# Gate columns from a stream with stationary weights, and softmax rows scaled on GpSimd in the neighbourhood attention

## The chip, the cores and the metric

The kernel runs on one core of a Trainium2 chip. The metric is device time in microseconds (us), median of the runs: 3284.68 us before (3 runs, 3283.81 to 3284.96). One further execution was profiled; the trace is of that one.

## What is computed

Two blocks follow one another on 256 tokens of width 2048, all in float32. The first is a transformer block (SwiGLU, grouped and differential attention, SwiGLU). The second has two layers; the change is in these. Layer 0 works on 256 image tokens and 256 context tokens (four tiles of 128 tokens), layer 1 updates only the image tokens (two tiles). What matters of the reference:

```python
p = h @ w_in                       # h: normed tokens; p holds pool, q, k, v, gate b, conv, gate c
s_loc = einsum(q_r, k_win) + bias  # 8 x 16 window, 16 heads of 64
s_ctx = einsum(q_r, kc)            # 256 context keys
p_ = softmax(concatenate([s_loc, s_ctx]))
na = einsum(p_loc, v_win) + einsum(p_ctx, vc)
yb = na * silu(p[..., OFF_B_G:OFF_C_U])          # the gate of the attention, 1024 columns
yc = conformer_conv(p[..., OFF_C_U:OFF_C_G]) * silu(p[..., OFF_C_G:])
x_new = x + gate * (concatenate([ya, yb, yc]) @ w_out)
```

The context tokens of layer 0 attend to the 256 context keys alone (no window).

## The kernel before

Every large product is done in three matmuls of a split float32 (fp32r): high activations by high weights, low by high, high by low. A weight piece is 128 x 512. `hi_piece` on ScalarE rounds it, `lo_piece` on VectorE makes the remainder, TensorE uses both. The ring has four pieces, and ScalarE and VectorE run two pieces ahead (`LOOK`). In `chunk_pieces` the activations are the stationary operand (128 x 128, `hT`) and the weights move (512 columns, lines 456, 457 and 461). One chunk has 16 pieces and yields 512 output columns for `nt` token tiles in `nt` PSUM banks.

In each layer `ly` of the second block the streams of `SEGS` come in the order q, k, v, g, two chunks each. `take4` (line 1779) copies each finished bank to `qkvg` (token rows, columns free); `tap` adds one tap of the depthwise convolution (line 1774) on VectorE for each piece. The gate g is thus held by token rows in `qkvg[:, 3]`. After the streams ScalarE, in its program order, turns the convolution's result into columns (four copies, line 1065, after the last taps), applies Silu to the whole gate (line 1071) and takes a square root (line 1073). TensorE runs some filling matmuls on `ones` (`fill`, line 1984), waits for the four copies (`cv_turned`) and transposes the convolution's result (line 2406). From there the layer norm of the convolution (VectorE line 1785 and on), the pointwise product (line 2425) and the attention follow.

The attention goes over 8 pairs of heads. A group `g` has two units `u = 2g, 2g+1`, one per head, for one tile of queries; a pair has three groups in layer 0 (`G = 3`; the third, `t == 2`, holds both context tiles, 256 queries) and two in layer 1 (`G = 2`). All engines run a hand-written software pipeline, one `step(g)` for each group:

- TensorE: `staged` for the next pair at one step in `G` (line 2437), `na_scores(g + 1)` (lines 2450 to 2459), `na_turn(2g)` and `na_turn(2g + 1)` (line 2471: the exponentials are transposed), `na_gate(g - 1)` (line 2481: the gate, already divided by the softmax sum, is transposed), `na_values(g - 1)` (lines 2493 and 2500).
- VectorE: `na_gate(g - 1)` (reciprocal of the sums, line 1834; gate times reciprocal, line 1837), `take_q` at one step in `G` (line 1801), `na_max(2g + 2)` and `na_max(2g + 3)` (lines 1817 and 1823: scores plus bias, row maximum), `na_out(g - 1)` (line 1846: copy of the transposed gate, line 1849: product with the values' result).
- ScalarE: `take_k` (line 1088), `na_exp(2g + 2)` and `na_exp(2g + 3)` (lines 1094 and 1099), `na_pt(2g)` and `na_pt(2g + 1)` (line 1108: transposed exponentials to SBUF).
- GpSimd issues DMAs and clears a few tiles (line 2662 clears `nil`, 128 x 256, just ahead of each attention). It has no part in the steps.

Each engine executes its queue in order. `na_turn(u)` waits for `p_made`, the exponential of its unit, and nothing else but a free PSUM bank. After the last group `o_hi` and `o_low` split the gated result into `hT` for the output stream `o2`.

Of the kernel before, what the change touches and what calls it, by code (L numbers as in the profile page):

```python
# [17 lines left out]
F32 = mybir.dt.float32  # L18
# [97 lines left out]
def build(nc, a, out, xs_dram):  # L116
    ctx = ExitStack()
    with ctx:
# [4 lines left out]
            ca_const_in glu_made gates_made yt_done yt_taken pl_done pl_taken py_done py_taken pad_made  # L123
            conv_step cf_in cf_done z_made cz_done s_made pw_done yc_made na_in bias_in nil_made rot_made
            st_dve pt_done pt_taken gs_done gs_taken x4r_in fin_in y_out gate_diag rs_made cf_sd zt_done zt_taken w_made og_in s_diag sbc_done mods_made y1_made sig_made ag_made gc_made hq_made tq_done tq_taken
            vw_in cv_turned tmp_made y_made gr_made gt_done gt_taken""".split()
# [52 lines left out]
        qkvg = at("qkvg", Q, [P, 4, 4, 2 * CH])  # L179
        ca = at("ca", Q, [P, 5, 4, CH])  # L180
# [82 lines left out]
        def phase(name, pieces, taken, groups, fulls=0, turns=None):  # L263
            phases[name] = Phase(*total)
            for k, n in enumerate((pieces, taken, groups, fulls, groups if turns is None else turns)):
# [20 lines left out]
                [("q", 0, 2, 2), ("k", 2, 2, 4), ("v", 4, 2, 4), ("g", 6, 2, 2)]]  # L286
# [114 lines left out]
        def head_rows(nt, n):  # L401

            k = kt_of(n) - 4
            return qkvg[:, 3, 0:nt, k * P:(k + 1) * P]

        def tok_tiles(v):

            return v.rearrange("p (t n) -> p t n", n=P)
# [282 lines left out]
        def _(act):  # L691
# [330 lines left out]
            for ly in range(2):  # L1022
# [36 lines left out]
                for k, (nm_, _, n_, _) in enumerate(SEGS[ly]):  # L1059
                    stream(phases[f"s{ly}{nm_}"].pieces, n_, after=gate_c if k == 0 else None)  # L1060

# [8 lines left out]
                act.wait_ge(S["acc_taken"], phases[f"mx{ly}"].taken)  # L1070
                act.activation(qkvg[:, 3, 0:nt], qkvg[:, 3, 0:nt], ACT.Silu).then_inc(S["gates_made"], 1)
# [61 lines left out]
                def o_hi(n, ly=ly, nt=nt):  # L1133
# [5 lines left out]
                    else:  # L1139
                        act.wait_ge(S["o_taken"], o_total(ly + 1))  # L1140
                        act.activation(tok_tiles(dst), head_rows(nt, n), ACT.Copy).then_inc(S["tg_hi"], 1)
# [43 lines left out]
        def _(dve):  # L1185
# [524 lines left out]
            for ly in range(2):  # L1710
# [55 lines left out]
                for nm_, c0, n_, snt in SEGS[ly]:  # L1766
# [9 lines left out]

                    def take4(i, t, c0=c0, nm_=nm_, snt=snt):
                        bank = acc[first_bank(snt, i + (nm_ == "q")) + t]
                        dve.tensor_copy(qkvg[:, c0 // 2, t, bass.ds(i * CH, CH)], bank[:]).then_inc(S["acc_taken"], 1)
# [47 lines left out]
                def na_gate(g):  # L1827

                    s, t = 2 * g % 4, kinds[2 * g % U][1]
                    n = 2 if t == 2 else 1  # L1830
                    dve.wait_ge(S["p_made"], 16 + u0 + 2 * g + 2)

                    wait(dve, "gr_made", v0 + g - 1)
                    link(dve.reciprocal(rr4[:, s:s + 2, 0:n], sm4[:, s:s + 2, 0:n]))
                    for k in range(n):
# [863 lines left out]
```

## Time and profile before

| | |
|---|---|
| median of 3 runs | 3284.68 us |
| the profiled execution | 3289.47 us |
| its span (first to last instruction) | 3287.6 us |
| granted TensorE clock, mean | 0.996 |
| stream g, layer 0 / layer 1 | about 87 us / 43 us |
| attention, layer 0 / layer 1 | 87.9 us (2443.1 to 2531.0) / 55.6 us (3125.9 to 3181.5) |

The times stand in microseconds from the start of the span. The profile names engines as PE (TensorE matmuls), PEld (weight loads), DVE (VectorE), ACT (ScalarE), POOL (GpSimd) and SP. A row names the line of the kernel, the operation, what is written and read, and the shape as partitions x elements. A float32 matmul that is not split appears as two rows of MATMUL (xcount is doubled), a split (fp32r) one or a transpose as one. Busy times of TensorE overlap, since matmuls are pipelined; the spacing of their starts says what one costs.

### The profile page before, as it was taken

The numbers are of one execution on the slowest core, as the hardware profiler recorded it, in microseconds if no ns is written. First come the engines' busy times: TensorE is split into PE (matmuls) and PEld (weight loads), VectorE is DVE, ScalarE is ACT, GpSimd is POOL, SyncE is SP. The second block draws the span as 40 slices with busy tenths as digits, with TensorE's granted clock in tenths as the row PEclk, the third lists the DMA queues.
The fourth block names the chain that finished last, engine by engine and source line by source line (L and its number), as shares of the span: only waits on it lengthen the run. The fifth ranks groups of instructions, "written<-read, shape, count | busy, mean of one in ns | idle before, by whom it ended". The sixth has DMA issues, their size and how long they took to land.

```text
span 3287.6 us, 41059 instructions
## 1 busy us (share of the span) xinstructions
PE 3235.8 (98%) x15334; PEld 2647.4 (81%) x15334; DVE 2262.9 (69%) x4132; ACT 1544.2 (47%) x2880; POOL 97.2 (3%) x186
## 2 busy tenths in 40 slices
PE   9999999999999999999999999999999999999998
PEld 7888888888888788888888788888866778888766
DVE  6888888877766788888877633556656337756666
ACT  6544454445665554455555522222246336522464
POOL 0000000000000000000000000000000000000000
PEclk9999999999999999999999999999999999999999
DMA  8888877776555788887887432333321235543625
GB/s 278 267 263 258 259 259 255 264 256 194 154 153 173 250 268 259 260 259 257 266 268 257 143 109 90 99 97 97 109 93 72 89 100 183 180 123 99 190 78 172
DMA packets 286023, 616.35 MB, mean 187 GB/s; under 512 B 18880, under 2 KB 21504, under 8 KB 284160
## 3 DMA queue, kind: packets, MB, share of 16 engines
q1 hardware_dynamic: 261792, 527.50, 50.2%
q0 software_dynamic: 22656, 82.78, 7.9%
q10 hardware_dynamic: 1376, 3.44, 0.3%
q8 instruction: 122, 2.00, 0.3%
q14 instruction: 77, 0.63, 0.1%
HBM read 605.26 MB, written 6.29 MB: 186 GB/s over the span
## 4 chain that ended last, share of the span: by engine, by line
PE 94%; DVE 2%; ACT 2%; DMA 2%; issue 1%; SPq 0%; ACTq 0%; DVEq 0%
PE acc L456 29%; PE acc L461 29%; PE acc L457 29%; PE tp L2471 1%; PE acc L2493 1%; PE tp L2425 1%; DMA raw<-ffn_w_gu 1%; PE tp L2034 1%; PE acc L2456 0%; PE cgw L2437 0%; DVE lo L451 0%; PE cgw L2187 0%; PE tp L1996 0%; PE cgw L2374 0%; PE cgw L2565 0%
## 5 line engine op out<-in xcount | busy, mean ns | idle before, releaser
L447 ACT ACTIVATE hi<-raw 128x512 fp32r<-128x512 f32 x1808 | 1134.0, 632 | 1551.2 <-PE acc L461 1438.2
L451 DVE TENSOR_TENSOR lo<-raw,hi 128x512 fp32r<-128x512 f32 x1808 | 1208.7, 689 | 835.4 <-ACT hi L447 826.3
L456 PE MATMUL acc<-hi,hT_hi 128*128 128x512 f32 x1760 | 696.5, 396 | 9.4 <-DVE hT_lo L1259 4.9
L457 PE MATMUL acc<-hi,hT_lo 128*128 128x512 f32 x1760 | 685.8, 390 | 0.0
L456 PE MATMUL acc<-hi,h_hi 128*128 128x512 f32 x1696 | 671.5, 396 | 7.9 <-ACT hi L447 4.5
L457 PE MATMUL acc<-hi,h_lo 128*128 128x512 f32 x1696 | 662.4, 391 | 0.0
L461 PE MATMUL acc<-lo,h_hi 128*128 128x512 f32 x1696 | 534.1, 390 | 0.9 <-DVE lo L451 0.9
L461 PE MATMUL acc<-lo,hT_hi 128*128 128x512 f32 x1760 | 514.5, 390 | 0.0
L456 PEld LDWEIGHTS acc<-hi,hT_hi 128*128 128x128 f32 x1760 | 330.7, 188 | 87.5 <-DVE hT_lo L1259 7.5
L461 PEld LDWEIGHTS acc<-lo,hT_hi 128*128 128x128 f32 x1760 | 331.0, 188 | 69.5
L457 PEld LDWEIGHTS acc<-hi,hT_lo 128*128 128x128 f32 x1760 | 330.9, 188 | 69.3 <-issue 2.6
L456 PEld LDWEIGHTS acc<-hi,h_hi 128*128 128x128 f32 x1696 | 319.6, 188 | 75.8 <-ACT hi L447 6.2
L461 PEld LDWEIGHTS acc<-lo,h_hi 128*128 128x128 f32 x1696 | 319.2, 188 | 69.1 <-DVE lo L451 1.3
L457 PEld LDWEIGHTS acc<-hi,h_lo 128*128 128x128 f32 x1696 | 319.8, 189 | 64.5
L456 PE MATMUL acc<-hi,uT_hi 128*128 128x512 f32 x704 | 275.3, 391 | 0.7 <-DVE lo L451 0.7
L457 PE MATMUL acc<-hi,uT_lo 128*128 128x512 f32 x704 | 274.0, 389 | 0.0
L1272 DVE CUSTOM_DVE_ANT_0 cgw<-mw,cb 128x1024 f32<-128x1024 f32 x192 | 235.5, 1227 | 1.1 <-DMA mw<-wmt 1.1
L1274 DVE CUSTOM_DVE_ANT_0 mw<-mw,cb 128x1024 f32<-128x1024 f32 x192 | 234.5, 1221 | 0.0
L461 PE MATMUL acc<-lo,uT_hi 128*128 128x512 f32 x704 | 220.0, 389 | 0.0
L1774 DVE SCALAR_TENSOR_TENSOR cv<-yT,dw,cv 128x512 f32<-128x512 f32 (+1 forms) x256 | 156.9, 613 | 0.0
L456 PEld LDWEIGHTS acc<-hi,uT_hi 128*128 128x128 f32 x704 | 132.2, 188 | 28.7 <-DVE lo L451 1.5
L461 PEld LDWEIGHTS acc<-lo,uT_hi 128*128 128x128 f32 x704 | 132.1, 188 | 27.8 <-DVE lo L451 0.2
(300 smaller groups left out, 2141.7 us busy)
## 6 DMA issues: line engine op xcount, KB each, us to landing
raw<-ffn_w_gu SPq DMA_DIRECT2D x352, 512.0 KB, 5.8
raw<-w_in SPq DMA_DIRECT2D x280, 512.0 KB, 3.8
raw<-ffn_w_down SPq DMA_DIRECT2D x176, 512.0 KB, 5.6
mw<-wmt POOLq DMA_DIRECT2D x132, 512.0 KB, 5.7
raw<-w_out SPq DMA_DIRECT2D x96, 512.0 KB, 4.3
mw<-wmt SPq DMA_DIRECT2D x60, 512.0 KB, 6.1
ball<-rpbx SPq DMA_DIRECT2D x8, 768.0 KB, 9.7
x<-x_rest SPq DMA_DIRECT2D x2, 2048.0 KB, 7.8
```

Of the source, the lines that this page charges most:

```text
L447: act.activation(hi[:, g % RING, :], raw_piece(g), ACT.Copy).then_inc(S["hi_made"], 1)
L451: dve.tensor_tensor(lo[:, g % RING, :], raw_piece(g), hi[:, g % RING, :].bitcast(F32), ALU.subtract).then_inc(S["lo_made"], 1)
L456: pe.matmul(bank, act_hi, hi[:, slot, :], start=start, stop=False)
L457: pe.matmul(bank, act_lo, hi[:, slot, :], start=False, stop=False)
L461: return pe.matmul(bank, act_hi, lo[:, slot, :], start=False, stop=stop)
L1272: dve.tensor_tensor_reduce(cgw[:].rearrange("p a n -> p (a n)"), w, c[:, 0], 1.0, 0.0, ALU.mult, ALU.add, dst[:, 0:1])
L1274: dve.tensor_tensor_reduce(w, w, c[:, 1], 1.0, 0.0, ALU.mult, ALU.add, dst[:, 1:2])\
L1774: dve.scalar_tensor_tensor(out=av, in0=yv, scalar=dw[:, ly, bass.ds(j * 16 + s, 1)], in1=av, op0=ALU.mult, op1=ALU.add).then_inc(S["conv_s ...
L2034: ins = pe.transpose(tp[f][:, k * L + t * P:k * L + (t + 1) * P], ub[:, t, (2 * f + k) * P:(2 * f + k + 1) * P], ident[:])
L2425: ins = pe.matmul(tp[t % 2][:], sT[:, t % 2, c * P:(c + 1) * P], cpw[:, c, :], start=(c == 0), stop=(c == 3))
L2471: ins = pe.transpose(tp[u % 2][:, j * P:(j + 1) * P], src, ident[:])
L2493: ins = pe.matmul(acc[2][e * NA_D:(e + 1) * NA_D, c0:c0 + w], qkvg[:, 2, 2 + j, cols[e]], pt[:, (2 * g + e) % 4, (j + local) * w:(j + loca ...
```

## The change

- The gate stream g is turned round: `turned_stream` takes 128 x 128 blocks of the weights as the stationary operand and moves the tokens, 512 columns in layer 0 and 256 in layer 1, so that the gate comes out by columns (feature rows, tokens free). Four PSUM banks are used in both layers. ScalarE empties each bank with Silu straight into a new tile `gT`; these instructions stand behind the `hi_piece` calls of their chunk and ahead of the four copies of line 1065. VectorE copies nothing in this stream, and the Silu over the whole gate is gone.
- In the attention `na_gate` is removed on TensorE and VectorE. VectorE's `na_roots(g)`, at the head of its step `g`, makes the reciprocals for group `g` (before: `g - 1`), and GpSimd multiplies the exponentials of each unit by them, in place (128 x 384; two times 128 x 256 for a unit of the context). `na_turn(u)` waits for that (`pr_made`) in place of `p_made`. `na_out` is one product of the values' bank and `gT`; the values use two PSUM banks in turn.

```diff
+                ph = phases[f"s{ly}g"]
+                for c in range(2):
+                    for j in range(LOOK, 16 + LOOK):
+                        hi_piece(act, ph.pieces + 16 * c + j)
+                    for b in range(4):
+                        bank_done(act, ph, 4, c, b)
+                        act.activation(gT[:, 4 * c + b, 0:nt * P], g_bank(nt, b), ACT.Silu).then_inc(S["acc_taken"], 1)
...
-                act.wait_ge(S["acc_taken"], phases[f"mx{ly}"].taken)
-                act.activation(qkvg[:, 3, 0:nt], qkvg[:, 3, 0:nt], ACT.Silu).then_inc(S["gates_made"], 1)
...
-                def na_gate(g):
...
-                    link(dve.reciprocal(rr4[:, s:s + 2, 0:n], sm4[:, s:s + 2, 0:n]))
-                    for k in range(n):
-                        gv = qkvg[:, 3, t + k, g // G * P:(g // G + 1) * P].rearrange("p (e d) -> p e d", d=NA_D)
-                        ins = dve.tensor_tensor(gv, gv, rr4[:, s:s + 2, k:k + 1].broadcast_to([P, 2, NA_D]), ALU.mult)
-                    ins.then_inc(S["gr_made"], 1)
+                def na_roots(g):
+
+                    v, n = 2 * g % 4, 2 if kinds[2 * g % U][1] == 2 else 1
                     dve.wait_ge(S["p_made"], 16 + u0 + 2 * g + 2)
...
+                    wait(dve, "pr_made", u0 + 2 * g - 2)
+                    dve.reciprocal(rr4[:, v:v + 2, 0:n], sm4[:, v:v + 2, 0:n]).then_inc(S["rr_made"], 1)
...
-                    dve.wait_ge(S["gt_done"], v0 + g + 1)
-                    dve.tensor_copy(block, tok_tiles(acc[3][:, cols])).then_inc(S["gt_taken"], 1)
+                    block = gT[:, g // G, t * P:(t + n) * P]
                     dve.wait_ge(S["o_done"], 12 + v0 + g + 1)
-                    dve.wait_ge(S["gt_taken"], v0 + g + 1)
-                    dve.tensor_tensor(block, tok_tiles(acc[2][:, cols]), block, ALU.mult).then_inc(S["o_taken"], 1)
+                    dve.tensor_tensor(block, acc[2 + g % 2][:, 0:n * P], block, ALU.mult)\
+                       .then_inc(S["o_taken"], 1)
...
                 def step(g):
                     p = g // G
-                    na_gate(g - 1)
+                    if g < 8 * G:
+                        na_roots(g)
...
                 for u in range(4):
                     na_max(u)
+                na_roots(0)
...
+            def turned_stream(ph, chunks, nt):
...
+                        w = hi[:, (p0 + j) % RING, b * P:(b + 1) * P]
+                        for h in range(2):
+                            pe.matmul(g_bank(nt, b), w, hT[h][:, kt_of(j), 0:nt * P], start=(j == 0 and h == 0), stop=False)
...
                 def na_turn(u):
-                    pe.wait_ge(S["p_made"], 16 + u0 + u + 1)
+                    pe.wait_ge(S["pr_made"], u0 + u + 1)
...
-                def na_gate(g):
...
-                    for k in range(2 if t == 2 else 1):
-                        ins = pe.transpose(acc[3][:, c0 + k * P:c0 + (k + 1) * P],
-                                           qkvg[:, 3, t + k, g // G * P:(g // G + 1) * P], ident[:])
-                    ins.then_inc(S["gt_done"], 1)
...
+                U, kinds = (6, 4)[ly], kinds_of(nt)
+                for u in range(8 * U):
+                    n, v = (2 if kinds[u % U][1] == 2 else 1), u % 4
+                    pool.wait_ge(S["rr_made"], (units + u) // 2 + 1)
+                    for k in range(n):
+                        cols = slice(k * L, NK if n == 1 else (k + 1) * L)
+                        ins = pool.tensor_scalar(pr[:, v, cols], pr[:, v, cols], rr4[:, v, k:k + 1], None, ALU.mult)
+                    ins.then_inc(S["pr_made"], 1)
```

## Rows read from the trace of the kernel before

**Rows 1.** The page's first part: busy time, share of the span, instructions.
```profile
PE 3235.8 (98%) x15334; PEld 2647.4 (81%) x15334; DVE 2262.9 (69%) x4132; ACT 1544.2 (47%) x2880; POOL 97.2 (3%) x186
```
**Rows 2.** Timeline (start, us, engine, line, operation): TensorE over one pair, layer 0.
```profile
2451.40 0.45 PE L2450 MATMUL acc<-Tk,Tq 64*64 64x128 f32 x8
...
2455.09 0.45 PE L2450 MATMUL acc<-Tk,Tq 64*64 64x128 f32 x8
...
2456.11 0.87 PE L2471 MATMUL tp<-ident,pr 128*128 128x128 f32 x6
2456.82 0.38 PE L2481 MATMUL acc<-ident,qkvg 128*128 128x128 f32 x2
2457.13 1.08 PE L2493 MATMUL acc<-pt,qkvg 128*64 128x256 f32 x8
...
2459.16 1.13 PE L2459 MATMUL acc<-Tk,Tq 64*128 64x256 f32 x8
2460.23 0.87 PE L2471 MATMUL tp<-ident,pr 128*128 128x128 f32 x6
2460.94 0.27 PE L2481 MATMUL acc<-ident,qkvg 128*128 128x128 f32 x1
2461.14 0.66 PE L2493 MATMUL acc<-pt,qkvg 128*64 128x128 f32 x8
...
2461.96 0.34 PE L2450 MATMUL acc<-Tk,Tq 64*64 64x128 f32 x4
```
**Rows 3.** Timeline, TensorE over one pair of layer 1.
```profile
3144.36 0.45 PE L2450 MATMUL acc<-Tk,Tq 64*64 64x128 f32 x8
...
3149.85 0.88 PE L2437 MATMUL cgw<-ident,qkvg 128*128 128x128 f32 x6
3150.66 0.34 PE L2450 MATMUL acc<-Tk,Tq 64*64 64x128 f32 x4
```
**Rows 4.** Groups by line and shape, layer 0's attention: busy us, mean ns | idle before.
```profile
L1099 ACT ACTIVATE pr<-pr,nm 128x256 f32<-128x256 f32 x32 | 15.9, 496 | 9.3 <-DVE nm L1823 9.3
...
L1823 DVE CUSTOM_DVE_ANT_0 pr<-acc,ball 128x256 f32<-128x256 f32 x32 | 11.7, 421 | 4.8 <-PE acc L2459 4.8
...
L1849 DVE TENSOR_TENSOR qkvg<-acc,qkvg 128x128 f32<-128x128 f32 x16 | 4.7, 292 | 5.1 <-PE acc L2500 4.3
...
L1834 DVE RECIPROCAL rr<-sm 128x2 f32<-128x2 f32 x16 | 2.5, 155 | 0.0
```
**Rows 5.** Groups by line and shape of GpSimd over the whole span.
```profile
L2662 POOL MEMSET ball<- 128x256 f32 x2 | 0.6, 312 | 137.8 <-DMA cpb<-conv_pw_b 137.8
...
L2691 POOL MEMSET const-float32-0.0<- 128x1 f32 x1 | 0.1, 93 | 0.2 <-issue 0.2
```
**Rows 6.** Timeline, the end of stream g in layer 0 and what follows.
```profile
2413.24 3.88 ACT L1065 ACTIVATE yT<-cv 128x512 f32<-128x512 f32 x4
...
2417.66 0.39 PE L461 MATMUL acc<-lo,hT_hi 128*128 128x512 f32 x1
...
2419.61 1.91 PE L2406 MATMUL acc<-ident,yT 128*128 128x128 f32 x16
```
**Rows 7.** Timeline, the same place in layer 1.
```profile
3108.31 2.05 ACT L1065 ACTIVATE yT<-cv 128x256 f32<-128x256 f32 x4
...
3111.96 1.04 PE L2406 MATMUL acc<-ident,yT 128*128 128x128 f32 x8
```
**Rows 8.** Groups by line from 2000 us on: Silu of one 128x512 tile on ScalarE.
```profile
L1058 ACT ACTIVATE gC<-ca 128x512 f32<-128x512 f32 x6 | 3.7, 616 | 0.0
```
**Rows 9.** Timeline, two following pieces of stream g in layer 1.
```profile
3096.18 0.61 PE L461 MATMUL acc<-lo,hT_hi 128*128 128x512 f32 x2
...
3097.54 0.61 PE L461 MATMUL acc<-lo,hT_hi 128*128 128x512 f32 x2
```
**Rows 10.** Stretches: length, then PE, PEld, DVE, ACT, POOL busy (x), PEclk, DMA, GB/s.
```profile
3128.00:3134.00 6.00, 3.55 (x36) 2.31 (x36) 2.45 (x11) 3.85 (x11) 0.00 (x0) 1.00 0.00 0
3134.00:3140.00 6.00, 6.00 (x52) 4.55 (x50) 3.16 (x12) 2.88 (x8) 0.00 (x0) 0.72 0.00 0
```

More of the change, by code:

```diff
@@ L179, in build @@
         qkvg = at("qkvg", Q, [P, 4, 4, 2 * CH])
+        gT = at("gT", Q + 48 * K1, [P, 8, 2 * L])
         ca = at("ca", Q, [P, 5, 4, CH])
@@ L1775, in tap @@
                                                  op0=ALU.mult, op1=ALU.add).then_inc(S["conv_step"], 1)
+                    if nm_ == "g":
+                        for i in range(n_):
+                            for j in range(LOOK, 16 + LOOK):
+                                lo_piece(dve, phases[f"s{ly}g"].pieces + 16 * i + j)
+                                tap(i, j - LOOK)
+                        break
                     def take4(i, t, c0=c0, nm_=nm_, snt=snt):
@@ L1901, in o_low @@
                     high, low = (h[:, kt_of(n), 0:nt * P] for h in hT)
-                    if n in O_TURNED:
-                        dve.tensor_tensor(low, o_bank(nt, O_TURNED.index(n)), high.bitcast(F32),
-                                          ALU.subtract).then_inc(S["tg_lo"], 1)
-                    else:
-                        dve.tensor_tensor(tok_tiles(low), head_rows(nt, n), tok_tiles(high.bitcast(F32)),
-                                          ALU.subtract).then_inc(S["tg_lo"], 1)
+                    src = o_bank(nt, O_TURNED.index(n)) if n in O_TURNED else head_rows(nt, n)
+                    dve.tensor_tensor(low, src, high.bitcast(F32), ALU.subtract).then_inc(S["tg_lo"], 1)
                 for n in range(LOOK):
@@ L2499, in na_values @@
                         for e in range(2):
-                            ins = pe.matmul(acc[2][e * NA_D:(e + 1) * NA_D, c0 + half * 64:c0 + half * 64 + 64],
+                            ins = pe.matmul(acc[2 + g % 2][e * NA_D:(e + 1) * NA_D, half * 64:half * 64 + 64],
                                             v_window(2 * t + half, cols[e]),
@@ L2636, in _ @@
                 gain_load(c)
+            units = 0
             for ly in range(2):
@@ L2662, in _ @@
                 pool.memset(nil, 0.0).then_inc(S["nil_made"], 1)
+                U, kinds = (6, 4)[ly], kinds_of(nt)
[6 more added lines that the diff above has]
+                    ins.then_inc(S["pr_made"], 1)
+                units += 8 * U
                 if ly == 0:
```

63 lines of the change are left out of this document (40 added, 23 removed).

## The prediction

> **What bounds the kernel now.** I read the page's first part first: TensorE is busy for 98% of the span, VectorE for 69%, ScalarE for 47%, GpSimd for 3% [rows 1]. So time is lost or won where TensorE's queue changes. The change touches three places, and each is read on TensorE's timeline by the spacing of starts, since modelled busy times overlap.
>
> In the gate stream TensorE never waits: the pieces of layer 1 follow at 1.36 us for six matmuls, 0.227 us each [rows 9]. In the attention a pair of heads takes 10.56 us in layer 0 (2451.40 to 2461.96) [rows 2] and 6.30 us in layer 1 (3144.36 to 3150.66) [rows 3]; there are eight pairs in each. Inside a pair the blocks stand nearly end to end: scores 1.02 us, six transposes 0.71, gate transposes 0.31, values of the context group with the staging after them 2.03, scores of the context group 1.07, gate transposes 0.20, values of a window group 0.82 [rows 2]. So TensorE's own work nearly sets the pair, and the exponentials, maxima and copies of the other engines fit beside it because every step works on other groups. In the convolution's tail the end is set by a serial chain that starts with TensorE's transposes of line 2406 [rows 6, 7].
>
> **The gate stream.** The count of columns moved is unchanged. In layer 0 there are as many matmuls of 512 columns as before: nothing. In layer 1, 192 matmuls of 512 columns become 384 of 256. No row shows such a matmul. If it took half of 0.227 us, the stream would stay at 43.5 us; six transposes of 128 columns, each with its own weight load, follow at 0.118 us [rows 2], so a load hardly holds the pair up below that. I take 0.118 x 384 = 45.3 us: +1.8 us. If 256 columns took as long as 512, it would be +43.5 us; the row of the transposes is much nearer, so I keep that end as a rival only. VectorE loses twelve copies here; TensorE didn't wait for them, so they gain nothing.
>
> **The tail after the stream.** The big Silu goes, but it ran while VectorE worked, so this is also nothing. What counts is ScalarE's order. The four copies of line 1065 ran under the last piece: 3.88 us from 2413.24 in layer 0, while the last matmul began at 2417.66 and ended 0.39 later, and TensorE transposed their result at 2419.61, after its filling matmuls [rows 6]. Now four Silus stand ahead of them, and the last can't start before the last bank is complete. In layer 0: 2418.05 + 0.62 (Silu of such a tile [rows 8]) + 3.88 = 2422.6 for line 2406, against 2419.61: +3.0 us, and the whole serial chain behind moves with it. In layer 1 the copies take 2.05 us, and TensorE's transposes came at 3111.96; with the distance of layer 0 (1.95 us) the last matmul began at 3110.01 and ended at 3110.40 [rows 6, 7]. Four Silus of 256 columns take about 0.5 us each (as the exponential of that shape, 0.496 [rows 4]), the last ending some 0.7 after the matmul: 3110.4 + 0.7 + 2.05 = 3113.15, +1.2 us. Sum of the tails: +4.2 us.
>
> **The attention, what is removed.** TensorE loses the gate transposes: 0.31 + 0.20 + 0.20 = 0.71 us for a pair of layer 0 and 0.40 of layer 1 [rows 2]. VectorE loses a gate product and a copy for each group. If nothing else happened, that would be worth 8 x 0.71 + 8 x 0.40 = 8.9 us.
>
> **What is added: a pass over the exponentials on GpSimd.** Its price isn't in the trace, as GpSimd only clears tiles: 93 ns for one element, 312 ns for 256 [rows 5]. The line through both is 0.86 ns per element. Clearing writes only. If the scale ran at that rate, 128x384 (call it a) would take 0.42 us and 128x256 (b) 0.31. If each element cost twice that, for one read and one write, a = 0.75 and b = 0.53. I take the middle, a = 0.60 and b = 0.43, and keep both ends, and a slower engine as a rival below.
>
> The Trainium skill, GPSIMD Engine Reference, section 3.1, puts a body of at most two operations at 1.03 cycles per element (0.86 ns at its 1.2 GHz); the trace's clearing agrees (0.86 ns). For two-input operations it gives 2.6 cycles, and section 4.1 advises VectorE for elementwise work. An estimate by that page: at 1.03 cycles the sum would be the low end below, about +6 us; at 2.6 cycles a would be 0.93, b 0.65 and the sum about +34.
>
> GpSimd itself isn't the bound: a pair of layer 0 costs it 4a + 4b = 4.1 us of over 10. But the pass stands in a chain that was shorter. `na_turn(u)` waited for an exponential made a step earlier; now it waits for exponential, reciprocal and scale. Behind that wait TensorE queues the values of group g-1, the staging and the scores of g+2. And `na_roots(g)` at the head of VectorE's step waits for the exponential of 2g+1, and behind it queue `take_q` and the maxima for g+1; ahead of it stands `na_out`, which waits for the values. No DMA stands behind GpSimd's waits before the next output stream. So I followed the longest loop over one pair of layer 0, with 0.1 us for each of six hops between engines (my choice; no row carries one, and at nothing the loop is 0.6 us shorter):
>
> - TensorE: values of the context group and staging 2.03, scores of the next context group about 1.0 [rows 2];
> - VectorE: first maxima, 2 x 0.42; ScalarE: four exponentials of 256, 4 x 0.496 = 1.98 [rows 4];
> - hop, reciprocal 0.16 [rows 4], hop, scales of both context units 4b, hop;
> - TensorE: four transposes 0.47 and values 0.82 [rows 2]; hop, `na_out` 0.29, reciprocal 0.16 [rows 4], hop, two scales 2a, hop, three transposes 0.36 [rows 2], and the values of the next context group begin.
>
> That is 8.71 + 2a + 4b: 11.63 us with my price, against 10.56. Eight pairs: +8.6 us. For layer 1 the loop goes over two groups: reciprocal 0.16, hop, 2a, hop, three transposes 0.36, values 0.82, staging 0.81 [rows 3], scores 1.02, six transposes 0.71, values 0.82 [rows 2], hop, `na_out` 0.29 [rows 4]: 5.29 + 2a = 6.49 against 6.30, eight pairs +1.5 us. At the start the first transposes wait for the four first maxima, a reciprocal and a scale where one exponential was enough (some 2 us later); at the end the last group's gate product, transposes and copy drop out of the chain (some 1.5 us). I put +0.5 us for each layer, +1.0.
>
> **The sum.** 1.8 + 4.2 + 8.6 + 1.5 + 1.0 = +17.1 us. Against the profiled execution (3289.47 us, its span 3287.6) that is 3306.6; that execution stands 4.8 us above the median of the runs, so on the median it is 3284.7 + 17.1 = 3302 us. Low end, a = 0.42, b = 0.31 and no extra in the stream: loops 10.79 and 6.13, so 1.8 - 1.4 + 1.0 + 4.2 = +5.6, 3290. High end of these prices, a = 0.75, b = 0.53: loops 12.33 and 6.79, so 14.2 + 3.9 + 1.0 + 4.2 + 1.8 = +25, 3310.
>
> **The rivals.**
> - *The scale is hidden and the transposes' gain shows* (not slower). It decides where the loop falls below TensorE's own work: 10.56 - 0.71 = 9.85 for a pair, which asks for 2a + 4b under 1.14 us, or a of about 0.23. Then layer 0 gains 5.7, layer 1 3.2, and with the tails and the stream (+6.0) the sum is -2.9: 3282 us, no change. For it speaks that GpSimd is idle and that its clearing is short; against it that a row of 256 cleared alone takes 0.31 [rows 5]. For a real gain the waits left in the pair would have to go too.
> - *GpSimd is much slower*, a = 1.0 and b = 0.7 or more: loops 13.51 and 7.29, so 23.6 + 7.9 + 1.0 + 4.2 + 1.8 = +38.5: 3323 us. By the page named above this is near its two-input rate. For it speaks that no row shows GpSimd reading; against it the clearing.
> - *TensorE's clock falls.* In layer 1, after a stretch in which TensorE was busy for 3.55 of 6 us, the granted clock of the next 6 us was 0.72 [rows 10], that is half clock (1.2 in place of 2.4 GHz) for some 3.4 us, which costs at most 1.7 us of work. The change adds such waits at the tail of layer 0 and at the start of each attention (a few us, inside my range). If it happened once in each pair of layer 0, it would be +14 on top: 3316 us. Against it: in steady state TensorE would still work 9.85 of 11.6 us.
> - *The moved tokens don't get cheaper with 256 columns* (the stream doesn't do what it says): +43.5 in place of +1.8, 3344 us.
>
> **How the numbers follow.** This kernel's measurement can tell about 0.2% (6.6 us) from no change. The forecast gets 58%, GpSimd slower 17%, the clock 8%, the 256 columns 2%; hidden or as cheap as clearing, and so within 0.2%, 11%; a gain beyond 0.2% 4%. That makes faster 0.04, same 0.12 (a little of the forecast's low end is with it), slower 0.84. The range goes from the low price of the scale to the slow GpSimd, 3289 to 3324.
>
> **What would show it.** In the profile of the changed kernel: GpSimd's scale of 128x384 near 0.6 us (64 of them) and of 128x256 near 0.43 (32); pairs at about 11.6 and 6.5 us by the starts of line 2450's scores; TensorE's idle time ahead of the transposes of `pr` put down to GpSimd; line 2406's transposes starting 4.6 us after the last matmul of stream g in layer 0 (1.6 before) and released by the four copies; layer 1's stream at 45 us. I am wrong if pairs of layer 0 stand below 10.3 us, if the copies run ahead of the last Silu, or if GpSimd's scale is below 0.3 us.

## The result, and the profile after

The changed kernel takes 3369.56 us (median of four runs, 3366.22 to 3372.28) against 3284.82 for the kernel before on the same chip: a ratio of 1.0256, 95% interval 1.0241 to 1.0270. It is slower by 85 us where +17 was forecast and 3324 was the upper end. The profiled execution of the changed kernel took 3372.28 us with a span of 3370.5, so 82.8 us more than the one before; the differences below are between these two executions. One execution of the last kernel in the table of experiments took 5455.65 us at a mean granted clock of 0.555 and is left out there.

The page's first part, and then the rows of the new pass from GpSimd's groups by line and shape (busy us, mean ns of one | idle time before):

```profile
PE 3277.9 (97%) x15478; PEld 2674.6 (79%) x15478; DVE 2231.9 (66%) x4032; ACT 1550.9 (46%) x2894; POOL 204.7 (6%) x282
```
```profile
L2695 POOL TENSOR_SCALAR pr<-pr,rr 128x384 f32<-128x384 f32 x64 | 78.8, 1242 | 115.1 <-DVE rr L1844 115.1
...
L2695 POOL TENSOR_SCALAR pr<-pr,rr 128x256 f32<-128x256 f32 x32 | 29.0, 923 | 21.7 <-DVE rr L1844 21.7
```

TensorE's busy time is 42 us higher than in [rows 1], though it lost the gate transposes: a sign that it ran slower, not that it had more to do. GpSimd's pass takes 1.242 and 0.923 us where 0.60 and 0.43 were forecast from the clearings [rows 5]; from start to start it is 1.23 and 0.905.

Where the 82.8 us lie, by landmarks on the timelines of both kernels (us):

| stretch | before | after | difference | forecast |
|---|---|---|---|---|
| start of the span to the last gate matmul, layer 0 | 2417.66 | 2414.23 | -3.4 | 0 |
| last gate matmul to the first scores, layer 0 | 25.5 | 28.8 | +3.3 | +3.0 |
| first scores to the last output product, layer 0 | 87.5 | 142.4 | +55.0 | +9.1 |
| gate stream, layer 1 | 43.5 | 46.0 | +2.5 | +1.8 |
| last gate matmul to the first scores, layer 1 | 15.9 | 16.7 | +0.8 | +1.2 |
| first scores to the last output product, layer 1 | 56.5 | 80.9 | +24.4 | +2.0 |

The sum is +82.6. So the stream and the tails came out as forecast, and the two attentions hold +79.4 of which +11.1 was forecast. From the third window scores of a layer to its last scores it is +45.7 and +16.0 us (layer 0 and 1), ahead of that (second to third) +5.0 and +3.6, behind it +4.3 and +4.9. In the first row the difference stands at 3.4 us already at 1965 us of the span, far ahead of all that the change touches; the same transposes stand between 1959.6 and 1963.2 us in the profiled executions of the twelve kernels with the turned stream, so such a difference is of the size of their spread. Two following matmuls of the new stream in layer 1:

```profile
3161.74 0.28 PE L2117 MATMUL acc<-hT_hi,hi 128*128 128x256 f32 x1
3161.86 0.28 PE L2117 MATMUL acc<-hT_lo,hi 128*128 128x256 f32 x1
```

The attention of layer 1 is the easier one to read, as TensorE's granted clock is 1.00 over the steps shown (0.95 from 3200 to 3245 us). GpSimd, VectorE and TensorE over one step (timelines: start, us, engine, line, operation, in brackets the idle time before and what ended it):

```profile
3208.83 2.46 POOL L2695 TENSOR_SCALAR pr<-pr,rr 128x384 f32<-128x384 f32 x2 [1.93 <-DVE rr L1844]
3213.22 2.46 POOL L2695 TENSOR_SCALAR pr<-pr,rr 128x384 f32<-128x384 f32 x2 [1.92 <-DVE rr L1844]
```
```profile
3208.37 0.29 DVE L1851 TENSOR_TENSOR gT<-acc,gT 128x128 f32<-128x128 f32 x1 [2.34 <-PE acc L2526]
3208.58 0.16 DVE L1844 RECIPROCAL rr<-sm 128x2 f32<-128x2 f32 x1
...
3212.76 0.29 DVE L1851 TENSOR_TENSOR gT<-acc,gT 128x128 f32<-128x128 f32 x1 [1.55 <-PE acc L2526]
3212.97 0.15 DVE L1844 RECIPROCAL rr<-sm 128x2 f32<-128x2 f32 x1
```
```profile
3211.35 0.55 PE L2507 MATMUL tp<-ident,pr 128*128 128x128 f32 x3 [0.67 <-POOL pr L2695]
3211.82 0.66 PE L2519 MATMUL acc<-pt,qkvg 128*64 128x128 f32 x8
3212.31 0.28 PE L2526 MATMUL acc<-pt,vw2a 128*64 128x64 f32 x4
```

Read it as a ring: reciprocal 3208.58, two scales until 3211.29, the second unit's transposes 3211.35, the values of the group before until 3212.7, their output product 3212.76, the next reciprocal 3212.97. The step is 2.46 + 1.93 = 4.39 us, and a pair of layer 1, two steps, 8.78, against 6.30 in [rows 3]. Every step holds a whole pass, two scales.

In layer 0 a pair takes 16.2 and 17.9 us in turn (by the starts of the context group's reciprocals), against 10.56 [rows 2]. There the clock falls as well. Stretches of one pair (length, then busy us of PE, PEld, DVE, ACT, POOL, the granted clock, DMA share, GB/s):

```profile
2473.00:2476.00 3.00, 2.38 (x31) 1.57 (x31) 1.84 (x11) 2.68 (x10) 0.33 (x2) 1.00 0.00 0
2476.00:2479.00 3.00, 1.07 (x4) 0.67 (x4) 0.54 (x4) 1.72 (x6) 3.00 (x4) 0.78 0.00 0
2479.00:2482.47 3.47, 3.10 (x28) 2.38 (x28) 0.36 (x2) 0.88 (x2) 0.32 (x1) 0.50 0.02 5
```

While GpSimd scales the four context rows (3.00 of 3.00 us busy) TensorE works for 1.07 us and its granted clock averages 0.78, and in the next 3.5 us it is 0.50: 1.2 in place of 2.4 GHz. The same values of a window group then take 1.12 us in place of 0.66.

The tail of layer 0 is as it was forecast. Timelines, ScalarE and TensorE:

```profile
2412.61 2.64 ACT L1067 ACTIVATE gT<-acc 128x512 f32<-128x512 f32 x4 [2.71 <-PE acc L2120]
2415.15 3.81 ACT L1072 ACTIVATE yT<-cv 128x512 f32<-128x512 f32 x4
```
```profile
2414.23 0.39 PE L2120 MATMUL acc<-hT_hi,lo 128*128 128x512 f32 x1
2414.46 1.89 PE L1984 MATMUL cgw<-dw,ones 128*128 128x256 f32 x8
2419.02 3.13 PE L2442 MATMUL acc<-ident,yT 128*128 128x128 f32 x16 [2.67 <-ACT yT L1072]
```

The transposes of yT start 4.79 us after the last matmul's start; in [rows 6] it was 1.95. They are released by the copies, and these stand behind the Silus.

Where each attention starts up, from the second window scores to the third, the clock is low too (before, it is 1.00 in both stretches):

```profile
2445.81:2456.25 10.44, 7.51 (x56) 5.53 (x57) 3.44 (x15) 4.49 (x14) 4.91 (x4) 0.67 0.00 0
3186.85:3194.74 7.89, 4.31 (x24) 2.79 (x24) 1.61 (x7) 3.69 (x11) 3.38 (x3) 0.55 0.00 0
```

### The profile page after: what moved, and what is told of

The parts are those of the page before. It is cut to its first block, busy times and chain, and to the rows that moved or that the text cites. A ratio compares the mean times of both kernels' runs of the same rounds, so it can differ in the third digit from the quotient of the medians.

```text
span 3370.5 us, 41319 instructions
## 1 busy us (share of the span) xinstructions
PE 3277.9 (97%) x15478; PEld 2674.6 (79%) x15478; DVE 2231.9 (66%) x4032; ACT 1550.9 (46%) x2894; POOL 204.7 (6%) x282
## 4 chain that ended last, share of the span: by engine, by line
PE 91%; POOL 2%; ACT 2%; DVE 2%; DMA 1%; issue 1%; SPq 0%; ACTq 0%; DVEq 0%
PE acc L456 27%; PE acc L461 27%; PE acc L457 27%; PE acc L2117 3%; POOL pr L2695 2%; PE acc L2120 1%; PE acc L2519 1%; PE tp L2507 1%; DMA raw<-ffn_w_gu 1%; PE tp L2461 1%; PE tp L2034 1%; PE cgw L2473 0%; DVE lo L451 0%; PE cgw L2221 0%; PE tp L1996 0%
## 5 line engine op out<-in xcount | busy, mean ns | idle before, releaser
L456 PE MATMUL acc<-hi,hT_hi 128*128 128x512 f32 x1568 | 621.5, 396 | 8.7 <-DVE hT_lo L1264 4.9
L457 PE MATMUL acc<-hi,hT_lo 128*128 128x512 f32 x1568 | 610.6, 389 | 0.0
L461 PE MATMUL acc<-lo,hT_hi 128*128 128x512 f32 x1568 | 457.1, 389 | 0.0
L456 PEld LDWEIGHTS acc<-hi,hT_hi 128*128 128x128 f32 x1568 | 294.4, 188 | 79.9 <-DVE hT_lo L1264 8.9
L457 PEld LDWEIGHTS acc<-hi,hT_lo 128*128 128x128 f32 x1568 | 294.6, 188 | 61.6 <-issue 2.6
L461 PEld LDWEIGHTS acc<-lo,hT_hi 128*128 128x128 f32 x1568 | 294.4, 188 | 61.5
```

The lines of the kernel that those rows point to most:

```text
L456: pe.matmul(bank, act_hi, hi[:, slot, :], start=start, stop=False)
L457: pe.matmul(bank, act_lo, hi[:, slot, :], start=False, stop=False)
L461: return pe.matmul(bank, act_hi, lo[:, slot, :], start=False, stop=stop)
```

## The experiments

The theory after the result (A): the pass's price, 2.46 and 3.62 us a step, stands in a ring of one step in which all else waits; the waits let TensorE's clock fall in layer 0; stream and tail are small. The rivals: the clock is most of it (C), the pass costs by its length wherever it stands (B), the rest of the change costs as much (E).

| run | median us | ratio to before (95%) | pair, layer 0 | pair, layer 1 |
|---|---|---|---|---|
| before | 3284.8 to 3286.0 | 1 | 10.56 | 6.30 |
| the change | 3369.6 | 1.0256 (1.0241 to 1.0270) | 16.2 to 17.9 | 8.8 to 9.3 |
| values first | 3330.7 | 1.0140 (1.0125 to 1.0155) | 12.3 to 15.2 | 6.96 |
| filler, long | 3392.2 | 1.0326 (1.0308 to 1.0343) | 17.49 | 11.35 |
| scale on VectorE | 3297.3 | 1.0036 (1.0023 to 1.0049) | 10.85 | 6.16 |
| no scale | 3288.6 | 1.0007 (0.9998 to 1.0017) | 10.24 | 6.08 |
| filler, short | 3358.5 | 1.0225 (1.0209 to 1.0240) | 15.06 | 8.9 to 9.9 |
| four forms (layer 1) | 3368.5, one execution | not compared | 16.2 to 18.0 | by form |
| half the columns | 3327.2 | 1.0132 (1.0115 to 1.0149) | 12.8 to 14.8 | 6.97 |
| convolution first | 3365.4 | 1.0246 (1.0230 to 1.0261) | 16.0 to 17.9 | 8.8 to 9.6 |
| product form | 3329.2 | 1.0136 (1.0122 to 1.0150) | 12.9 to 14.7 | 7.06 |
| product, values, convolution first | 3300.3 | 1.0046 (1.0032 to 1.0059) | 11.02 | 6.10 |
| VectorE by unit | 3293.9 | 1.0028 (1.0018 to 1.0037) | 10.80 | 6.25 |
| before, copies of pt between | 3286.1 | 1.0002 (0.9993 to 1.0011) | 10.50 | 6.30 |

Pairs are taken from start to start of the same reciprocal in neighbouring pairs; the first two and the last of each layer are left out. For the scale on VectorE by unit, where the reciprocals come singly, they are taken by the output products (layer 0) and the scores (layer 1).

**No scale** (layout of the change without the pass):

```
-                    pe.wait_ge(S["pr_made"], u0 + u + 1)
+                    pe.wait_ge(S["p_made"], 16 + u0 + u + 1)
```

with GpSimd's loop and the wait for it in `na_roots` taken out.

> Edit: the scale is left out (the rows of the softmax are not normalised) and the turns wait for the exponentials as before the change; the turned gate stream, the Silus and the shorter chain of the output stay. It shows what the rest of the change costs or gives. Theory A: pairs at TensorE's own 9.85 and 5.9 us, -5.7 and -3.2 us over the two layers, against +2.5 for the stream and +4.1 for the tails: 3281 to 3285 us. Rival E (the rest of the change costs as much as the pass, by stream or tail): 3300 us or more.

3288.6 us: the pass and what follows from it are worth 81 of the 85 us, so E falls. But there is no gain in the total either, and A's 3281 to 3285 is missed by 4 us. TensorE lost 0.71 us of transposes in a pair of layer 0 and the pair fell by 0.32 only (10.56 to 10.24), in layer 1 by 0.22 of 0.40. TensorE's waits of this run from 2455 to 2515 us, some six pairs (what waited for whom: us in total, times, the longest):

```profile
PE tp L2506 <- ACT pt L1113: 3.6, 5, 0.7
```

It waits up to 0.7 us in a pair for ScalarE's copy of a transposed unit, which stands behind four exponentials, and it did so in the kernel before (3.5 us in the same stretch). So TensorE's own work alone was not the bound that the 98% of [rows 1] seemed to say.

**Scale on VectorE** (GpSimd's loop moved behind the reciprocal):

```
-                    dve.reciprocal(...).then_inc(S["rr_made"], 1)
+                    link(dve.reciprocal(rr4[:, v:v + 2, 0:n], sm4[:, v:v + 2, 0:n]))
+                    for u in (2 * g, 2 * g + 1):
+                        for k in range(n):
+                            ...
+                            ins = dve.tensor_scalar(pr[:, u % 4, cols], ..., rr4[:, u % 4, k:k + 1], None, ALU.mult)
+                        ins.then_inc(S["pr_made"], 1)
```

> Edit: the same scale by VectorE, right behind its reciprocals; GpSimd does none. VectorE's price is not known; the output product on the same engine, 0.29 us for 128x128 and 0.42 for 128x256, would put 128x384 at 0.56 and 128x256 at 0.42. Theory A (the size of the pass decides): the one-step loops become 2 x 0.56 + 1.9 = 3.0 us in layer 1, below TensorE's own, so pairs about 6.0 to 6.4 us, and 8.71 + 1.12 + 1.68 - 0.2 = 11.3 us in layer 0: 3284.8 + 6 + 0 + 6.6 = about 3292 to 3300 us. Rival B' (any pass in that place costs what GpSimd's does, because the wait for a reciprocal is what holds the step): near 3350 us or more.

3297.3 us, inside A's 3292 to 3300; B' falls. The pair of layer 0 is below A's 11.3. The same instruction on the other engine (groups by line and shape):

```profile
L1847 DVE TENSOR_SCALAR pr<-pr,rr 128x384 f32<-128x384 f32 x64 | 24.0, 418 | 1.1
...
L1847 DVE TENSOR_SCALAR pr<-pr,rr 128x256 f32<-128x256 f32 x32 | 9.1, 350 | 0.3
```

Two of 384 columns take 0.75 us together and four of 256 take 1.14, a third of GpSimd's 2.46 and 3.62, and a pair takes 10.85 and 6.16 us. The granted clock is 1.00 throughout the pairs (2455 to 2520 us).

**Half the columns**:

```
                         cols = slice(k * L, NK if n == 1 else (k + 1) * L)
+                        cols = slice(cols.start, cols.start + (cols.stop - cols.start) // 2)
```

> Edit: GpSimd scales only the first half of each row (128x192 and 128x128); the rest is left as it is, so half the softmax is not normalised. From 1.242 us for 384 columns and 0.923 for 256 the line gives 0.76 for 192 and 0.60 for 128, which is what was once forecast for whole rows at the slow end. Theory A (a loop with 2a + 4b in layer 0, 2 x (2a + 1.93) in layer 1, clock kept): pairs 8.71 + 1.52 + 2.40 = 12.6 and 6.9 us; against the kernel without a scale (3288.6; pairs 10.24 and about 6.1) 8 x 2.4 + 8 x 0.8 = 25 us more, 3310 to 3318 us. Rival C (once TensorE waits at all its clock falls): 17 to 20 us more, about 3332. Rival H (GpSimd's price doesn't follow the columns): near 3369.

The rows took 0.765 (192 columns) and 0.606 us (128), as the line said, and layer 1 took 6.97 a pair where 2 x (2a + 1.93) gives 6.9. Layer 0 took 12.8 to 14.8, not 12.6, at a granted clock of 0.87, so the total of 3327 stands between A and C: the ring is right, and the clock comes on top in layer 0. These prices are near the high end of the forecast (0.75 and 0.53), for which my sum was 3310; with the measured prices put in it is 3313. So at a price that I had nearly allowed for, some 14 us would have been missed all the same.

**Filler, long and short** (work for TensorE while it waits; 3, then 1, in layer 0 alone):

```
-                    pe.wait_ge(S["pr_made"], u0 + u + 1)
                     pe.wait_ge(S["pt_taken"], max(u0 + u - 1, 0))
+                    fill(tp[u % 2], 3 if u > 1 else 0)
+                    pe.wait_ge(S["pr_made"], u0 + u + 1)
```

> Edit: three filling matmuls (0.23 us each at full clock, into the bank that the turn will use) ahead of each wait for a scaled unit, so that TensorE works while it waits; the order and all waits stay. It tells apart how much of the loss is the half clock. Theory A (waits in the loop first, the clock on top): the granted clock of the pairs goes to 1.00 and a pair of layer 0 to the loop's 14.6 to 14.8 us in place of 17.0, layer 1 stays at 8.8: 8 x 2.3 = 18 us less, some 3350 us. Rival C (the half clock is most of the loss): pairs near 11.6, some 3320 us or below. Rival D (the filling work itself lengthens the loop): 3370 us or more.

The long one gave what D said, 3392 us, and settled nothing else: a filling matmul is two pieces and takes 0.47 us, not 0.23, so six times three of them are 8.4 us of a pair, TensorE never waited for GpSimd, and the pair became 17.49 us of its own work.

> Edit: one filling matmul (two pieces, about 0.47 us) ahead of each wait for a scaled unit, in layer 0 alone. With three of them TensorE was at full clock but never waited for GpSimd, because the filling itself took 8.4 us of a pair; now it takes 2.8, and TensorE's work is 10 + 2.8 = 12.8 us. Theory A (in layer 0 the 17.0 us of a pair are a loop of about 14.8 at full clock, and the half clock on top): the granted clock of the pairs is 1.00 and a pair takes 14.5 to 15.2 us, so 8 x 2 = 16 us less than the changed kernel, 3350 to 3356 us. Rival F (the loop itself is 17 us long and TensorE's slow work is hidden in its waits): pairs stay at 17 and the time at 3366 to 3372. Rival G (so little filling doesn't hold the clock): granted clock below 0.9 and no gain.

```profile
2464.00:2494.00 30.00, 25.91 (x227) 16.88 (x225) 11.15 (x46) 16.08 (x47) 17.12 (x16) 1.00 0.01 2
```

With the short one the granted clock over 30 us of the attention is 1.00 and every pair takes 15.05 to 15.06 us. The total is 3358.5, 11 us below the change (16 forecast, and 2.5 above A's range); in the profiled executions layer 0's attention is 14.7 us shorter, 127.7 in place of 142.4. The filling is not in the ring, as one group of this run shows (TensorE's two fillings without a wait, then VectorE, ScalarE and GpSimd):

```profile
2471.22 0.70 PE L1984 MATMUL tp<-dw,ones 128*128 128x256 f32 x2
2472.08 0.60 PE L1984 MATMUL tp<-dw,ones 128*128 128x256 f32 x2
2473.87 0.29 DVE L1851 TENSOR_TENSOR gT<-acc,gT 128x128 f32<-128x128 f32 x1 [1.09 <-PE acc L2526]
2474.02 0.18 ACT L1104 ACTIVATION_READ_ACCUMULATOR pr<-pr,nm 128x1 f32 x1
2474.24 0.18 DVE L1844 RECIPROCAL rr<-sm 128x4 f32<-128x4 f32 x1
2474.51 3.63 POOL L2695 TENSOR_SCALAR pr<-pr,rr 128x256 f32<-128x256 f32 x4 [2.21 <-DVE rr L1844]
```

The context group's reciprocal comes after the last exponential (until 2474.20), which the filling doesn't delay; the output product behind the filling is done at 2474.16, just before. After the other four fillings of the pair TensorE still waits for GpSimd, 0.16 to 0.93 us. So in layer 0 the ring at full clock is 15.05 us (14.8 by the loop of the prediction with the measured price), 4.5 above the pair of before, and the half clock adds 2 us on average: the smaller part. C falls as the main cause, F and G too.

**Values first** (TensorE makes the values of group g-1 before it waits for GpSimd's group g):

```
+                    na_values(g - 1)
                     for u in (2 * g, 2 * g + 1):
                         if g < 8 * G:
                             na_turn(u)
-                    na_values(g - 1)
```

> Edit: in TensorE's step the values of group g-1 stand ahead of the two turns of group g, not behind them. Theory A (the 1.24 us pass sits in a loop of one step: reciprocal, two scales, transposes, values of the group before, output product, next reciprocal; layer 1 shows it as 2 x 1.23 + 1.93 = 4.39 us a step): the values no longer wait for GpSimd, the loop spans two steps, and a pair is set by TensorE's own work (9.9 us in layer 0, 5.9 in layer 1) or by GpSimd's own 8.54 and 4.92: pairs of 9.9 to 10.6 and 5.9 to 6.4 us, about 3284.8 + 2.5 (stream) + 4.1 (tails) - 5 to +1 = 3286 to 3293 us. Rival B (the pass costs by its duration wherever it stands): pairs stay near 17.0 and 8.78, 3365 to 3370 us. Rival C (TensorE's clock is the cost, set off by the tail and not by the waits): the granted clock in the pairs of layer 0 stays near 0.7 and pairs near 14, about 3330 us.

39 us less than the change, so the order matters and B falls; but the time is 38 to 45 us above A's range. It is the time that C named, 3330, by another way: layer 1's pairs fell to 6.96 us, and the granted clock is 0.89 from 2455 to 2545 us, not 0.7. A second ring lay close behind. TensorE, GpSimd and VectorE's next reciprocal in layer 1 of this run:

```profile
3201.09 0.55 PE L2507 MATMUL tp<-ident,pr 128*128 128x128 f32 x3 [0.65 <-POOL pr L2695]
3201.47 0.82 PE L2473 MATMUL cgw<-ident,qkvg 128*128 128x128 f32 x6
3202.22 0.45 PE L2486 MATMUL acc<-Tk,Tq 64*64 64x128 f32 x8
```
```profile
3198.57 2.47 POOL L2695 TENSOR_SCALAR pr<-pr,rr 128x384 f32<-128x384 f32 x2 [1.86 <-DVE rr L1844]
3201.20 2.47 POOL L2695 TENSOR_SCALAR pr<-pr,rr 128x384 f32<-128x384 f32 x2 [0.17 <-DVE rr L1844]
3205.53 2.46 POOL L2695 TENSOR_SCALAR pr<-pr,rr 128x384 f32<-128x384 f32 x2 [1.86 <-DVE rr L1844]
```
```profile
3205.27 0.17 DVE L1844 RECIPROCAL rr<-sm 128x2 f32<-128x2 f32 x1 [0.69 <-ACT pr L1099]
```

Now the next scores stand behind the turns that wait (scale ends 3201.04, turn 3201.09, scores 3202.22), and behind them maxima, exponentials, reciprocals and the pass at 3205.53. This ring goes over two steps with one pass in it: 2.47 + 4.49 = 6.96 us a pair. I had looked for the next bound only in TensorE's and GpSimd's own sums.

**Four forms of the pass** (layer 1 only):

```
+                        form = 0 if ly == 0 else 1 + u // 2 % 4
...
+                            ins = pool.tensor_scalar(t, t, 0.5, None, ALU.mult)
...
+                            ins = pool.tensor_copy(t, t)
...
+                            ins = pool.tensor_tensor(t, t, t, ALU.mult)
```

> Edit: in layer 1 the pass over a unit is made in four forms in turn, on the same 128x384 elements: scale by a constant, plain copy, product of two tiles, and three scales of 128x128; layer 0 keeps the scale by a pointer. In layer 1 the result is not normalised. It measures the disputed price by itself. Theory A (a fixed 0.28 us and 2.5 ns per element for any pass with one read and one write): constant and copy 1.24 us, three thirds 3 x 0.60 = 1.8 us, the product longer. Rival J (the scalar that is read from memory is the cost): constant and copy at 0.42 to 0.75 us. Rival K (VectorE's work beside it slows GpSimd): the same form spreads over more than 0.1 us.

```profile
L2698 POOL TENSOR_SCALAR pr<-pr,rr 128x384 f32<-128x384 f32 x32 | 39.4, 1242 | 66.6 <-DVE rr L1844 66.6
...
L2708 POOL TENSOR_SCALAR pr<-pr,rr 128x128 f32<-128x128 f32 x24 | 14.0, 603 | 7.8 <-DVE rr L1844 7.8
L2700 POOL TENSOR_SCALAR pr<-pr 128x384 f32<-128x384 f32 x8 | 9.2, 1167 | 22.1 <-DVE rr L1844 22.1
L2704 POOL TENSOR_TENSOR pr<-pr 128x384 f32<-128x384 f32 x8 | 6.4, 826 | 9.1 <-DVE rr L1844 9.1
L2702 POOL COPY pr<-pr 128x384 f32<-128x384 f32 x8 | 3.8, 504 | 9.6 <-DVE rr L1844 9.6
```

A was wrong on the copy and on the product, J on the pointer. A copy takes 0.50 us, near the 0.60 of the forecast; a product of two tiles 0.83; a scale by a scalar 1.24, and with a constant still 1.17. So the cost sits in the scalar form, not in the reading (J falls), and all eight of a form lie within 0.02 us of each other (1.157 to 1.172, 0.501 to 0.508, 0.821 to 0.827), so no effect of VectorE's work beside it shows in these eight (K falls). From 128 to 384 columns a scale grows by 0.64 us: 2.5 ns per element and 0.28 fixed.

**Product form** (the same scale, with the reciprocal as a second tile that doesn't step):

```
-                        ins = pool.tensor_scalar(pr[:, v, cols], pr[:, v, cols], rr4[:, v, k:k + 1], None, ALU.mult)
+                        root = rr4[:, v, k:k + 1].broadcast_to([P, cols.stop - cols.start])
+                        ins = pool.tensor_tensor(pr[:, v, cols], pr[:, v, cols], root, ALU.mult)
```

> Edit: GpSimd makes the same scale as a product of two tiles, the second being the reciprocal read again and again along the row, in place of a scale by a scalar; order and waits stay. In the run with the four forms the product of two full tiles took 0.82 us for 128x384, the scale by a constant 1.17 and the copy 0.50. Theory A (the price of the form is the mis-sized term): 128x384 near 0.82 and 128x256 near 0.6 us, so pairs of layer 1 of 2 x (1.63 + 1.93) = 7.1 us and of layer 0 some 13 to 14 (15.05 at full clock less 0.83 for 2a less 1.2 for 4b, plus what the clock takes), 3322 to 3335 us. Rival L (an operand read with no step costs as much as the scalar): 1.2 us, no change from 3369 us.

```profile
L2696 POOL TENSOR_TENSOR pr<-pr,rr 128x384 f32<-128x384 f32 x64 | 51.6, 827 | 108.2 <-DVE rr L1844 108.2
L2696 POOL TENSOR_TENSOR pr<-pr,rr 128x256 f32<-128x256 f32 x32 | 18.6, 614 | 25.8 <-DVE rr L1844 25.8
```

As A said: 0.827 and 0.614 us, 7.06 us a pair of layer 1, 3329 us. One line of the pass is worth 40 of the 85 us; L falls.

**Convolution first** (the four copies ahead of the Silus of the last chunk):

```
+                    for k in range(4 if c else 0):
+                        act.wait_ge(S["conv_step"], 132 * ly + 129 + k)
+                        act.activation(by_columns(k, nt)..., cv[:, k, 0:nt * P]..., ACT.Copy).then_inc(S["cv_turned"], 1)
                     for b in range(4):
                         bank_done(act, ph, 4, c, b)
```

> Edit: ScalarE makes the four copies of the convolution's output ahead of the four Silus of the last gate chunk, not behind them. Theory A (the tail's +2.8 and +0.8 us come from the copies' place in ScalarE's queue): TensorE's transposes of yT begin about 2 us after the last matmul of the stream, as before the change, not 4.79 and 2.70; 3369.6 - 3.6 = 3366 us, less than the total can tell, so the trace decides. Rival I (VectorE's last taps or the banks of the stream hold the tail): the distance stays at 4 us or more.

```profile
2412.77 0.39 PE L2119 MATMUL acc<-hT_hi,lo 128*128 128x512 f32 x1
2413.00 1.89 PE L1983 MATMUL cgw<-dw,ones 128*128 128x256 f32 x8
2414.73 1.91 PE L2441 MATMUL acc<-ident,yT 128*128 128x128 f32 x16
```

The distance is 1.96 us again in place of 4.79, the transposes follow the filling matmuls without a wait, and the first scores of layer 0 come 25.5 us after the last gate matmul, as before the change. So the place in ScalarE's queue was the whole cost of this tail; in layer 1 it was 0.55 of the 0.8 us (16.13 in place of 16.68, before 15.89). The total is 4 us less, which it can hardly tell from its own spread.

**The causes taken away together, and two more.** First product form, values first and convolution first in one kernel:

> Edit: the product form on GpSimd, the values ahead of the turns, and the convolution's copies ahead of the last Silus, together. With the values first a pair of layer 1 was 6.96 us, a loop of two steps with one pair of passes in it, so 6.96 - 0.83 = 6.1; a pair of layer 0 was 12.33 where the clock held, so 12.33 - 0.83 - 1.2 = 10.3 to 10.9. Theory A (the three named causes are the whole loss): against the kernel without a scale (3288.6 us, pairs 10.24 and 6.08) +1 to +5 in layer 0, about 0 in layer 1, -3.6 in the tails: 3286 to 3293 us, that is as before the change within its measurement. Rival C (the clock falls as soon as TensorE waits at all): 3300 us or more.

3300.3 us, 69 of the 85 us back, with a granted clock of 1.00 in the pairs of layer 0 (2455 to 2525 us). The pairs of layer 1 are 6.10 as counted and those of layer 0 11.02, just above the 10.3 to 10.9, but the total is 7 above A's range, at the 3300 of C. From the second scores to the third, where each layer's attention starts up, it takes 9.9 and 6.9 us against 7.1 and 4.3 without a scale: the first passes have nothing beside them, and the granted clock in these stretches is 0.66 and 0.61 against 0.76 and 1.00. I had left that out; how much of it is the clock (C's cause, at the start alone) was not taken apart.

Then the scale on VectorE, unit by unit, with convolution first and ScalarE's exponentials and copies in turn:

> Edit: VectorE makes reciprocal and scale of each unit as soon as its own exponential is there (not of both units after the second), ScalarE alternates exponentials and copies of pt, and the convolution's copies stand ahead of the last Silus. With VectorE's scale a pair of layer 0 was 10.85 us and TensorE waited 1.1 us in it for the second scale. Theory A: that wait falls by about a unit's scale, pairs of 10.2 to 10.5 and about 6.1 us, tails -3.6: 3297 - 3.6 - 4 = 3287 to 3291 us, no better than before the change. Rival M (the pass can be hidden and the removed gate transposes then show): pairs below 9.9, 3281 us or less.

3293.9 us, some 3 us above A's range and 3 below the first VectorE version, still slower than before: 10.80 us a pair in layer 0, with 0.7 us of it TensorE's wait for the scale, and 6.25 in layer 1, where the first VectorE version had 6.16. M falls, the pass isn't hidden there either.

Last, ScalarE's turn-about alone, in the kernel before:

```
-                    for u in (2 * g + 2, 2 * g + 3):
-                        if g + 1 < 8 * G:
-                            na_exp(u)
-                    for u in (2 * g, 2 * g + 1):
-                        if g < 8 * G:
-                            na_pt(u)
+                    for e in range(2):
+                        if g + 1 < 8 * G:
+                            na_exp(2 * g + 2 + e)
+                        if g < 8 * G:
+                            na_pt(2 * g + e)
```

> Edit in the kernel before the change: ScalarE alternates exponentials of group g+1 and copies of pt of group g, where it made both exponentials first. In the kernel before TensorE waits 0.7 us in each pair of layer 0 for the copy of pt behind four exponentials, and so does the kernel without a scale; that wait would explain why leaving out the gate transposes gave 0.3 us a pair in place of 0.71. If so, pairs of 10.56 - 0.3 to 10.56 - 0.7 us in layer 0, 3279 to 3283 us. Rival N (the exponentials made later take the place of that wait): pairs stay at 10.5 or more and the time within 0.1% of before.

3286.1 us, 1.0002 (0.9993 to 1.0011): the wait for the copies is 0.5 us in place of 0.7 and the pair 10.50 in place of 10.56, against the 9.9 to 10.3 expected. This is rival N's outcome; its reason, that the exponentials made later take the wait's place, is argued and not shown. None of the kernels run here beats the kernel before.

## Why the prediction was wrong, point by point

The eight pairs of the sums below reach into the starts and ends of the attentions, so the shares don't add up to the 85 us.

- *The stream*: right. The matmuls of 256 columns in layer 1 follow at 0.120 us (forecast 0.118), and the stream takes 46.0 us, +2.5 for +1.8. The rival of 256 columns as dear as 512 is out.
- *The tails*: right in cause and size, 2.84 and 0.74 us by the transposes' starts where 3.0 and 1.2 were said, and confirmed by the run that turned the order round.
- *The price of the pass* is the step that failed: "a = 0.60 and b = 0.43", measured 1.23 and 0.905, twice that, and above even the rival's 1.0 and 0.7. The line through two clearings [rows 5] says what a write costs; the middle between that and its double, 0.60, was a fair value for a copy (0.50 measured), but the operation was a scale, and no row showed one. With the measured price the loops on record, 8.71 + 2a + 4b and 5.29 + 2a, give 14.8 and 7.75 us: 8 x 4.2 + 8 x 1.45 = +45 us in the pairs, where +10 was forecast.
- *The loop of layer 0* held: 14.8 by that sum, 15.05 us at full clock with the short filler.
- *The loop of layer 1* was a mistake of mine: I let it go over two groups with one pass, 7.75 us at the measured price. TensorE's values of g-1 stand behind the turns of g, and `na_out(g-1)` ahead of the next `na_roots`, both named in the prediction, and together they close the ring within one step: 2 x (2.46 + 1.93) = 8.78, as measured. At the forecast price that ring would have been 2 x (1.20 + 1.93) = 6.26, no longer than the pair of [rows 3], so the mistake cost nothing as long as the price was low.
- *The clock* was put at 8%, with "+14 on top" if it fell once in each pair of layer 0. That is what happened, at about that size: 17.0 against 15.05 us, 8 x 2 = 16 us (the run with the short filler was 11 us faster as a whole). It was argued away with TensorE working 9.85 of 11.6 us; with the pass at its real price that would be 9.85 of 15.
- *Start and end of the attentions*: 0.5 us each was forecast. From the second scores to the third it takes 10.4 and 7.9 us in place of 5.5 and 4.3, +5.0 and +3.6, and from the last scores to the last output product 13.4 and 11.8 in place of 9.1 and 7.0, +4.3 and +4.9: there the passes have nothing beside them, and the granted clock is between 0.55 and 0.75 where it was 1.00 before. The share of each was not taken apart.
- *The gain of the removed transposes*, 8.9 us, was there by about half: without any scale the pairs fell by 0.32 and 0.22 us, some 4.3 us in all, and with the stream's and the tails' +6.6 the kernel is as fast as before, to within 0.2%. "TensorE's own work nearly sets the pair" left out its wait for the copy of the exponentials.
- The Trainium skill, GPSIMD Engine Reference, sections 3.1 and 4.1, names about 2.6 cycles per element for a two-input operation and advises VectorE for elementwise work. The estimate made from it, +34 us, was nearer than my sum, but by luck: the rate belongs to another form, which took 0.83 us here and not the scale's 1.24. The advice agrees with the run on VectorE (418 against 1242 ns). Its 1.03 cycles for a body of at most two operations don't hold for this scale, whose 2.5 ns per element is 3.0 cycles at the page's 1.2 GHz; the measurement decides.

Left open: why a scalar makes GpSimd's pass dearer than a second tile, how the starts and ends divide between the passes and the clock, and the 3.4 us by which the changed kernel is ahead at 1965 us, in a part of the program that is the same.

## What to carry to other kernels

Before a pass is moved to an engine, find a row of that very operation on that engine; a clearing or a copy is no stand-in for a scale, and where there is none, let the bound be several times the nearest row. Then follow each ring that the new wait closes through the order of the queues, the shortest first (what stands behind the waiting instruction, and what that releases), and put the pass into it as often as it occurs. A busy share of 98% doesn't say that taking work from the engine gains: look for the waits inside the period first.

## What the runs showed of the hardware

- GpSimd on fp32 in SBUF, 128x384: copy 0.50 us, product of two tiles 0.83, scale by a pointer 1.24 and by a constant 1.17. The product with a second operand that doesn't step costs what the product of full tiles costs (0.827 and 0.826). VectorE's scale of the same tile takes 0.42.
- TensorE's granted clock fell from 1.00 to 0.50 within a pair, across a stretch with 1.07 of 3.00 us of work; one filling matmul of 0.47 us ahead of each wait held it at 1.00 over 30 us in which TensorE was busy for 25.9.
- A matmul of 256 columns follows the next at 0.120 us with its own weights, one of 512 at 0.227 [rows 9]: halving the moving columns costs 6% here, not 100%.
